# Both heads of a pair at once: scores, turns and dense matmuls of the attention in fewer, longer groups

## The reference, cut to what matters

```python
def hybrid_layer(x, ...):
    h = rms_norm(x, g_pre_mix)
    z = h @ w_in
    q, k, v, zu, zv = jnp.split(z, [D_ATTN, 2 * D_ATTN, 3 * D_ATTN, 3 * D_ATTN + D_SGU], axis=-1)
    ...
    attn = dilated_attention(q, k, v, rel_bias).reshape(B, S, D_ATTN)
    sgu = spatial_gating(jax.nn.gelu(zu), jax.nn.gelu(zv), sgu_ln_g, sgu_ln_b, sgu_w, sgu_b)
    mix = jnp.concatenate([attn, sgu], axis=-1) @ w_out
```

## Time and profile before

| | |
|---|---|
| median of 3 runs | 1688.92 us (1688.7 to 1689.56) |
| profiled execution, its own time | 1689.87 us |
| span of its trace | 1687.8 us |
| TensorE matmul busy | 1679.1 us, 99% of the span |
| VectorE / ScalarE / GpSimd busy | 74% / 48% / 25% |
| TensorE clock granted | 0.999 of full speed |

### The profile page before, as it was taken

How to read it: one execution, slowest core, us unless ns; L and a number is a source line. 1 busy time by engine, 2 the same in 40 slices (tenths; PEclk the granted TensorE clock), 3 DMA queues, 4 the chain that set the end, 5 groups by cost and what they waited for, 6 DMA issues and landing times.

```text
span 1687.8 us, 29256 instructions
## 1 busy us (share of the span) xinstructions
PE 1679.1 (99%) x9774; PEld 1468.6 (87%) x9774; DVE 1242.8 (74%) x2276; ACT 810.6 (48%) x1429; POOL 424.0 (25%) x217
## 2 busy tenths in 40 slices
PE   9999999999999999999999999999999999999998
PEld 7877788999998888889999998888888889999997
DVE  5656579888887878688688686576675598688685
ACT  5566563333332534754353354565655554343354
POOL 3332320000001497320220213432523310220221
PEclk9999999999999999999999999999999999999999
DMA  7542223333333233233332333231222233332331
GB/s 210 123 107 79 75 74 101 95 106 100 99 99 99 81 114 104 72 100 108 105 120 81 102 109 101 82 94 50 87 62 76 65 112 111 101 124 75 100 113 50
DMA packets 160146, 163.16 MB, mean 97 GB/s; under 512 B 10659, under 2 KB 126999, under 8 KB 160063
## 3 DMA queue, kind: packets, MB, share of 16 engines
q1 hardware_dynamic: 155599, 159.19, 31.1%
q10 hardware_dynamic: 4464, 2.89, 0.6%
HBM read 158.36 MB, written 3.67 MB: 96 GB/s over the span
## 4 chain that ended last, share of the span: by engine, by line
PE 93%; POOL 3%; DVE 1%; issue 1%; ACT 0%; DMA 0%; SPq 0%; DVEq 0%; POOLq 0%; ACTq 0%
PE ps L2000 36%; PE ps L2459 21%; PE ps L2484 10%; PE ps L2338 7%; PE ps L2363 6%; PE ps L2028 2%; PE ps L2566 1%; POOL wlo L1002 1%; PE ps L2039 1%; PE ps L2221 1%; PE ps L2240 1%; POOL wsum L1045 1%; POOL first_table L1008 0%; DMA lnmult<-const_lnmult 0%; PE ps L2204 0%
## 5 line engine op out<-in xcount | busy, mean ns | idle before, releaser
L1002 POOL TENSOR_TENSOR wlo<-raw,whi 128x1024 fp32r<-128x1024 f32 x60 | 145.2, 2436 | 588.4 <-ACT whi L1489 292.6
L2000 PE MATMUL ps<-h_hi,wlo 128*128 128x512 f32 x608 | 247.4, 407 | 0.1
L2000 PE MATMUL ps<-h_hi,whi 128*128 128x512 f32 x608 | 237.8, 391 | 0.0
L2000 PE MATMUL ps<-h_lo,whi 128*128 128x512 f32 x608 | 237.6, 391 | 0.0
L1124 ACT ACTIVATE whi<-raw 128x1024 fp32r<-128x1024 f32 x120 | 124.5, 1053 | 115.2 <-PE ps L2000 101.2
L2000 PE MATMUL ps<-m_hi,wlo 128*128 128x512 f32 x384 | 152.7, 398 | 0.3 <-POOL m_lo L1066 0.3
L2000 PE MATMUL ps<-m_hi,whi 128*128 128x512 f32 x384 | 149.7, 390 | 0.0
L2000 PE MATMUL ps<-m_lo,whi 128*128 128x512 f32 x384 | 149.7, 390 | 0.0
L2000 PEld LDWEIGHTS ps<-h_hi,whi 128*128 128x128 f32 x608 | 114.1, 188 | 25.3
L2000 PEld LDWEIGHTS ps<-h_hi,wlo 128*128 128x128 f32 x608 | 114.4, 188 | 22.2 <-issue 0.8
L2000 PEld LDWEIGHTS ps<-h_lo,whi 128*128 128x128 f32 x608 | 114.5, 188 | 20.9 <-issue 0.5
(11 more groups left out here) (506 smaller groups left out, 4931.6 us busy)
## 6 DMA issues: line engine op xcount, KB each, us to landing
raw<-in_ffn_w SPq DMA_DIRECT2D x264, 256.0 KB, 2.9
raw<-in_w_ff SPq DMA_DIRECT2D x128, 256.0 KB, 2.9
raw<-in_hg_w_in SPq DMA_DIRECT2D x64, 256.0 KB, 3.1
raw<-in_w_in SPq DMA_DIRECT2D x40, 256.0 KB, 4.8
raw<-in_cp_w_in SPq DMA_DIRECT2D x24, 256.0 KB, 2.9
raw<-in_w_out SPq DMA_DIRECT2D x16, 256.0 KB, 2.9
raw<-in_cp_w_out SPq DMA_DIRECT2D x16, 256.0 KB, 2.8
raw<-in_hg_w_out SPq DMA_DIRECT2D x16, 256.0 KB, 2.7
```

The source lines that it names most:

```text
L1002: pool.tensor_tensor(wlo[:, u % RING, :, :], raw[:, u % RING, :, :], whi[:, u % RING, :, :].bitcast(F32), ALU.subtract).then_inc(unit_lo, 1)
L2000: mm = pe.matmul(ps[:, b, :], wt[:, s, a, m * P:(m + 1) * P], xt[:, kts[a], :], start=starts and a == 0 and i == 0, stop=last)
```

## The change

The heads of a pair go together: score index i now means head `i % 2`, queries `i // 2`. `scores(t, p)` makes both heads' scores for the same 128 queries, four matmuls in the order k_lo of both, then the rounded k of both, into banks 4 and 5. Then come two turns side by side, and then one long dense part: 4, 8, 8, 8, 3 and 1 tiles in the loop, 6, 7, 7, 8, 3, 1 in the first pair, 3, 6, 6, 7, 2 in the last. ACT and DVE work in the same paired order. The matmuls are the same ones. Both heads' q and k are now rounded before the next pair's first scores, and ACT does both heads before turns 6 and 7.

```diff
 ACT
                 def turned(i):
-                    e, t, b = i // 4, i % 4, 6 + i % 2
+                    e, t, b = i % 2, i // 2, 6 + i % 2
...
+                def weights_behind(i):
+                    turned(i)
+                    weights(i + 2)
+                    turned(i + 1)
+                    weights(i + 3)
+
                 weights(0)
+                weights(1)
...
-                weights(7)
-                units(3)
-                drain_head("qkv", following, following + 1, 0)
+                weights_behind(4)
+                units(3 if following is not None else 2)
+                if following is not None:
+                    drain_head("qkv", following, following + 1, 0)
+                    drain_head("qkv", following, following + 1, 1)
                 turned(6)
                 turned(7)
-                drain_head("qkv", following, following + 1, 1)
-                drain_values("qkv", following)
+                if following is not None:
+                    drain_values("qkv", following)
 TensorE
-            def scores(i, p):
-                e, t = i // 4, i % 4
+            def scores(t, p):
+
+                heads = [banks.bank("att", ("s", 2 * t + e)) for e in range(2)]
                 cols = slice(t * P, (t + 1) * P)
-                b = banks.bank("att", ("s", i))
                 if t == 0:
-                    pe.wait_ge(qk_hi, p * 6 + (3 * e + 3))
+                    pe.wait_ge(qk_hi, p * 6 + 6)
                     pe.wait_ge(k_zero, 2)
-                    pe.wait_ge(qk_lo, p * 4 + (2 * e + 2))
-                pe.wait_ge(drained[b], before("att", ("s", i), p))
-
-                pe.matmul(ps[:, b, :], q_parts[:, e, cols], k_lo[:, e, :], start=True, stop=False)
-                pe.matmul(ps[:, b, :], q_parts[:, e, cols], k_his[:, e, :], start=False, stop=True).then_inc(filled[b], 1)
+                    pe.wait_ge(qk_lo, p * 4 + 4)
+                for e, b in enumerate(heads):
+                    pe.wait_ge(drained[b], before("att", ("s", 2 * t + e), p))
+                for k, begins, ends in ((k_lo, True, False), (k_his, False, True)):
+                    for e, b in enumerate(heads):
+                        mm = pe.matmul(ps[:, b, :], q_parts[:, e, cols], k[:, e, :], start=begins, stop=ends)
+                        if ends:
+                            mm.then_inc(filled[b], 1)
...
-                       cuts=(0, 2, 4, 6, 8, 10, 12, 14, 16, 18, 20, 22, 24, 28, 30, 31, 32)):
+            def attend(p, piece, before_it, following=None, cuts=(0, 4, 12, 20, 28, 31, 32)):
...
                 dense(0)
-                for i in range(6):
-                    scores(i + 2, p)
-                    dense(1 + 2 * i)
-                    turn(i)
-                    if i < 5:
-                        dense(2 + 2 * i)
-                dense(12)
+                for t in range(1, TT):
+                    scores(t, p)
+                    turn(2 * t - 2)
+                    turn(2 * t - 1)
+                    dense(t)
                 turn(6)
-                dense(13)
                 turn(7)
-                dense(14)
+                dense(4)
                 if following is not None:
                     scores(0, following)
-                    dense(15)
-                    scores(1, following)
+                    dense(5)
...
 DVE
             def biased(i, p):
-                e, t = i // 4, i % 4
+                e, t = i % 2, i // 2
...
                 if p:
                     scaled_weights(0, p)
+                scaled_weights(1, p)
                 u_cube(p)
...
+                for i in (2, 4, 6):
+                    biased(i, p)
+                    biased(i + 1, p)
                     scaled_weights(i, p)
-                    biased(i + 1, p)
-                scaled_weights(7, p)
+                    scaled_weights(i + 1, p)
...
                 if p + 1 < PAIRS:
                     qk_low(0, p + 1)
+                    qk_low(1, p + 1)
                     dve.wait_ge(btab_in[p + 1], 16 * (P // COPIES))
                     biased(0, p + 1)
-                    qk_low(1, p + 1)
                     biased(1, p + 1)
```

More of the change, by code:

```diff
@@ L1306, in attend @@
                 act.activation(ug[:, :], ps[:, 3, :], ACT.Copy).then_inc(u_ready, 1)
[L1307 to L1326, removed]
-                    weights(7)
-                    turned(6)
-                    turned(7)
-                    return
@@ L1331, in attend @@
-                values_copied()
-                weights(1)
                 if before_it is not None:
                     pair_high(before_it)
-                turned(0)
-                units(0)
+                values_copied()
+                if following is not None:
+                    units(0)
+                weights_behind(0)
                 u_tangent()
[L1338 to L1341, removed]
+                units(1 if following is not None else 0)
@@ L1342, in attend @@
+                weights_behind(2)
                 gate_high()
[L1343 to L1351, removed]
-                units(3)
-                drain_head("qkv", following, following + 1, 0)
+                units(2 if following is not None else 1)
+                weights_behind(4)
+                units(3 if following is not None else 2)
@@ L2223, in values @@
                 mm.then_inc(filled[7], 1)
-            def attend(p, piece, before_it, following=None,
-                       cuts=(0, 2, 4, 6, 8, 10, 12, 14, 16, 18, 20, 22, 24, 28, 30, 31, 32)):
+            def attend(p, piece, before_it, following=None, cuts=(0, 4, 12, 20, 28, 31, 32)):
                 def dense(n):
@@ L2265, in head_units @@
                 unit(U_QKV + j0, j, h_hi, h_lo, (2 * j, 2 * j + 1), "qkv", up_tags, j == 0, j == 3, turn, per,
-                     (2, 0, 1, 3) if behind_mixes else (0, 1, 2, 3), use=turn + (j0 // 4 - 1), part=part)
+                     (2, 0, 1, 3) if behind_mixes else (0, 1, 2, 3), use=turn + (j0 // 4 - 1), part=part,
+                     by_tile=True if behind_mixes else None)
             order = ((4, 5), (0, 1), (6, 7), (2, 3))
@@ L2285, in _ @@
             scores(0, 0)
-            scores(1, 0)
             mixes((2, 3))
-            attend(0, lambda j, part: head_units(4, j, part), None, 1)
+            attend(0, lambda j, part: head_units(4, j, part), None, 1, (0, 6, 13, 20, 28, 31, 32))
             with pe.Fori(0, PAIRS - 2) as r:
                 attend(r + 1, lambda j, part: head_units(8, j, part, r, 4), r, r + 2)
-            attend(PAIRS - 1, wout_early, PAIRS - 2, None, (0, 2, 4, 5, 7, 8, 10, 11, 13, 14, 15, 16, 17, 20, 21, 24))
+            attend(PAIRS - 1, wout_early, PAIRS - 2, None, (0, 3, 9, 15, 22, 24))
             values(PAIRS - 1)
@@ L2942, in attend @@
                     scaled_weights(0, p)
+                scaled_weights(1, p)
                 u_cube(p)
-                scaled_weights(1, p)
                 if p:
                     pair_low(p - 1)
[L2947 to L2954, removed]
-                    scaled_weights(i, p)
-                    biased(i + 1, p)
-                scaled_weights(7, p)
+                for i in (2, 4, 6):
+                    biased(i, p)
+                    biased(i + 1, p)
+                    scaled_weights(i, p)
+                    scaled_weights(i + 1, p)
+                    if i == 2:
+                        sgu_out(p)
+                    if i == 4:
+                        sgu_low(p)
                 if p + 1 < PAIRS:
                     qk_low(0, p + 1)
+                    qk_low(1, p + 1)
                     dve.wait_ge(btab_in[p + 1], 16 * (P // COPIES))
                     biased(0, p + 1)
-                    qk_low(1, p + 1)
                     biased(1, p + 1)
```

## The result

| | before | changed |
|---|---|---|
| median of 12 runs | 1689.42 us | 1692.74 us |
| range | 1688.6 to 1690.57 us, and one of 8139.65 | 1691.82 to 1694.18 us |
| span of the profiled execution | 1687.8 us | 1690.2 us |
| stretch from the first mixing matmul to the last pair's `values` | 129.52 us | 132.97 us |

The ratio of the changed kernel to the one before is 1.0021, interval 1.0013 to 1.0029: about 3.5 us slower. One execution of the kernel before took 8139.65 us; it counts in the median of 12 and is left out of the ratio. The forecast was 1691.4 us, +2.5, and within 0.2% of before; the ratio lies 0.01% over that bound, and its interval reaches to both sides of it.

What follows compares the result with a forecast made beforehand. The prediction took TensorE's own stream to bound the attention. A 3.6 us loss between pairs less 1.1 us of gains gave +2.5 us, forecast 1691.4 us, range 1688.4 to 1693.6.

Steps and rivals of the forecast that it cites:

- What bounds the kernel: In the attention, TensorE's own instruction stream sets the time; reordering gains only at seams and one short wait.
- The wait between pairs: Next pair's first scores wait for both heads' q and k: 1.2 us at three passages, 3.6 us, bounds 3.2 to 4.2.
- The refund of 0.1: At each passage, 0.1 us of the 1.30 us lateness taken back, because a load normally runs a matmul ahead.
- The gain of the longer runs: Fewer, longer dense runs lose less behind seams: 0.9 us gained, bounds nothing to 2.0; about 1.1 with turn 7.
- the wait at turn 7: Last pair's turn 7 waited for DVE's probabilities; seven dense tiles now stand ahead, so 0.15 us is gained.
- seams between kinds: Where TensorE changes kind of matmul, the first dense matmuls run slower, losing 0.047 to 0.065 us per run.
- Turns side by side gain nothing in themselves: Two adjacent turns save nothing: transposes cost 0.110 us each, 0.44 for four, 0.88 for eight.
- The other waits: Within rounds, ACT and DVE need 4.0 us after scores; TensorE returns after 6.4, in the last pair 4.8: no cost.
- second rival: Score banks empty too late at eight places, 0.7 us each: +5.6 us more, 1697 us; chance 0.06.
- the signs that I had set down: Forecast wrong if passage waits are absent or under 0.8 us, `scores(2)` or `scores(3)` wait, or dense pace differs from 0.229 us.
- The sum: Whole kernel: 3.6 us lost between pairs less 1.1 gained, +2.5 us, forecast 1691.4 us.
- The bank-rotation rule: Independent matmul groups should rotate through different banks, one evacuated while the next is computed; by it the new order is worse.

Runs made afterwards that it cites:

- the kernel of 128.49: Changed kernel with k finished before q, both heads' parts interleaved, and ACT's unit rounding moved so POOL rests during the gate's products: stretch 128.49 us, ratio 0.9994.
- the turns apart: Changed kernel with each round as turn, half the dense part, turn, other half: stretch 135.21 us, one run of 1695.15 us.
- the scores apart: Kernel of 128.49 us stretch, with two dense tiles between the two heads' scores of a round: stretch 130.02 us, one run of 1691.40 us.
- POOL away: Changed kernel with ACT's rounding of weight units moved, so POOL rests while DVE makes the gate's products: stretch 132.24 us, ratio 1.0018.
- the passage as before: Changed kernel with the old order between pairs: first head's scores wait for it alone, ACT copies turns between heads; stretch 137.12 us, ratio 1.0054.

## Why the prediction was right in its main steps and wrong in one, point by point

- **What bounds the kernel**: right. Where TensorE does not wait, the chain holds nothing but its own stream, and the two turns of the loop agree to 0.01 us (33.62 and 33.61 before).
- **The wait between pairs**: right in mechanism, place and price. Forecast 3 x 1.2 = 3.6 us; undoing it in the changed kernel gave 3.86, making it in the kernel before cost 3.69. The term is 0.1 to 0.3 short: 1.24 and 1.27 in the loop, 1.34 in the first passage, where TensorE's load came 0.19 us behind DVE's end in place of 0.05 (why it does there is not shown). The refund of 0.1 that I took was about right in the loop.
- **The gain of the longer runs**: 1.1 us forecast with the wait at turn 7, 1.03 measured. The size was right, its reason only in part, so some of that agreement is luck. I put all of it down to seams between kinds, at 0.047 to 0.065 each; pulled apart alone, a seam cost 0.025. The three seams of a loop turn are worth 0.08 us and the scores' three places 0.05 to 0.08, out of 0.28 to 0.27; the fourth seam (turns 6 and 7) and the fourth place (the next pair's first scores) were in neither test. From one pair of scores to the next within the loop, the same work (4 score matmuls, 8 transposes, 24 dense) takes 7.28 to 7.30 us in the kernel of 128.49, 7.30 or 7.31 with the turns apart, 7.31 to 7.34 with the scores apart, and 7.36 or 7.37 before. So both pulled apart at once, as before, cost some 0.07 us, more than the two alone, 0.02 and 0.03. That no run between two changes is then long enough to reach the steady 0.227 us would fit, but I have only argued it.
- **Turns side by side gain nothing in themselves**: right, 0.87 us for eight.
- **The other waits: "Both hold, by 2.1 and 0.8 us, so I cost it at nothing"**: this step failed in the last pair. The chain of 4.0 us was summed from rows and left out the gate's products, which DVE does ahead of the next bias; at 0.7 us each (the second rival's 1.4) they would have ended before the next scores were there, as they did with POOL away. The new order let POOL's subtraction start just ahead of the second product, which then took 2.86. With 18 matmuls in the round it reached TensorE: 0.73 us. It is the place of my second rival (the banks empty too late), in one of its eight places and for another cause; its long rounds held. By the signs that I had set down, a wait at `scores(3)` meant that the forecast was wrong here.
- **The sum**: +3.86 (three waits) + 0.62 (POOL) - 1.03 (paired rounds) = +3.45 us, the whole difference between 129.52 and 132.97; it must be, since the three are steps from one kernel to the next. (The 0.62 is the last turn's 0.72 less 0.10 in the others. In pair 0's turn the four first scores of the next pair take 1.06 us in place of 0.94. With the scores apart, under the same order of ACT's units, they take 0.91 there, so it need not be the units' doing; the cause is open.) Forecast was +2.5. The missing 1 us is POOL for the larger part, and the size of the wait for the rest.

The bank-rotation rule that I weighed and set aside (the Trainium skill, "Perfetto Trace Analysis") would, taken for the two score banks alone, have made the paired rounds themselves slow; with the waits removed they are faster than the old ones (128.49 us against 129.52), since dense matmuls in other banks run while these two are emptied. The rule that I should have looked up stands elsewhere: the Trainium skill's page "SBUF — State Buffer", section "SBUF: two separate sides", says that VectorE with two SBUF inputs and a GpSimd instruction that reads SBUF take one shared pair of ports as an exclusive lock, and that whichever comes second waits for the other's whole instruction. By that rule the product takes what is left of POOL's 2.38 or 2.39 us and its own 0.69 or 0.68: 3.00 us when it starts 0.07 us behind POOL, 2.40 when 0.67 behind. The trace agrees but for 0.12 to 0.14 us: 2.86 and 2.28. That the one waits for the other is what the runs show; that a lock on ports is behind it is the page's account.

## What to carry to other kernels

When work of two units is paired, the first consumer of the pair waits for the later one. Its slack must be counted from the last part of the second unit, not of the first: 0.5 us of slack in the earlier trace rows became a wait of 1.3. Finish the input with the longer chain first; here k ahead of q bought back all 3.9 us with the same instructions. And a new order moves other engines' work too: for each VectorE operation that reads two SBUF operands, look at what GpSimd does at its new time.

## What the runs showed of the hardware that I had not expected

A longer wait may cost TensorE its clock. In the kernel with the passage as before, the third wait of 2.3 us was followed by `values` at 5.12 us in place of 3.58. Its stretches from 160 to 180 us (from:to, us, then busy of PE, PEld, DVE, ACT, POOL, clock, DMA):

```profile
160.00:168.00 8.00, 7.68 (x38) 6.10 (x36) 3.09 (x7) 5.41 (x11) 2.40 (x1) 1.00 0.20 66
168.00:170.40 2.40, 0.81 (x4) 0.38 (x6) 1.43 (x3) 1.64 (x4) 0.00 (x0) 0.93 0.01 3
170.40:175.50 5.10, 5.10 (x17) 1.41 (x17) 3.29 (x8) 1.78 (x4) 0.00 (x0) 0.70 0.00 0
175.50:180.00 4.50, 4.50 (x28) 3.90 (x27) 1.77 (x5) 1.62 (x3) 0.00 (x0) 1.00 0.00 0
```

The granted clock was 0.70 of full speed on the mean there, that is partly at the lower level of 1.2 GHz (0.50 from 170.4 to 173, 1.00 again from 174), after TensorE had been busy for 0.81 of 2.40 us. `values` took 1.54 us longer. The two earlier waits of the same length had no such fall, nor had the waits of 1.2 to 1.35 us in any kernel here. So one fall in three is what this run shows; it was not repeated, and that the wait brought it about is not shown.
